# Scatter products of a mixture-of-experts tail on two PSUM banks, the output stored in quarters, the overflow flag read ahead of the loop

## The reference

```python
def moe_swiglu(h, w_router, w_gate, w_up, w_down):
    logits = (ht @ w_router).astype(jnp.float32)
    top_vals, top_idx = lax.top_k(logits, TOP_K)
    gates = jax.nn.softmax(top_vals, axis=-1)
    ...
    g = lax.ragged_dot(xs, w_gate, group_sizes)
    u = lax.ragged_dot(xs, w_up, group_sizes)
    y = lax.ragged_dot(jax.nn.silu(g) * u, w_down, group_sizes)
    y = y * gates.reshape(-1)[order][:, None].astype(y.dtype)
    out = jax.ops.segment_sum(y, tok, num_segments=t)
...
x = x + moe_swiglu(h, *p["ffn"])
```

## Time and profile before

| | |
|---|---|
| Median of 3 runs | 1593.89 us (1590.03, 1593.89, 1594.02) |
| Profiled execution, its own time | 1592.94 us |
| Profiled execution, span from first to last instruction | 1591.2 us |
| PE matmul busy | 1499.9 us (94%) |
| PE weight loads busy | 1205.7 us (76%) |
| DVE busy | 1151.8 us (72%) |
| ACT busy | 952.2 us (60%) |
| DMA, mean over the span | 268 GB/s |
| Largest share of the chain of waits | PE, line 646, 64% |

### The profile page before, as it was taken

How to read it: one execution, slowest core, us unless ns; L and a number is a source line. 1 busy time by engine, 2 the same in 40 slices (tenths; PEclk the granted TensorE clock), 3 DMA queues, 4 the chain that set the end, 5 groups by cost and what they waited for, 6 DMA issues and landing times.

```text
span 1591.2 us, 20133 instructions
## 1 busy us (share of the span) xinstructions
PE 1499.9 (94%) x7597; PEld 1205.7 (76%) x7597; DVE 1151.8 (72%) x1196; ACT 952.2 (60%) x922; POOL 68.3 (4%) x93
## 2 busy tenths in 40 slices
PE   6988979999887799999999999999999999999996
PEld 3677579999643578878878887887887887887884
DVE  6683225445254388888888888888888988888885
ACT  4323134444243377777777777776777767777773
POOL 2640000000010000000000000000000000000000
PEclk8998989999999799999999999999999999999997
DMA  7343924537430369989989999999999998998990
GB/s 235 113 42 97 350 106 162 183 109 262 159 106 1 106 237 368 375 307 364 372 326 345 372 339 336 368 337 337 369 337 336 369 371 304 367 375 308 363 367 28
DMA packets 197936, 425.92 MB, mean 268 GB/s; under 512 B 19331, under 2 KB 28385, under 8 KB 197857
## 3 DMA queue, kind: packets, MB, share of 16 engines
q1 hardware_dynamic: 197584, 425.23, 75.4%
q10 hardware_dynamic: 304, 0.06, 0.0%
HBM read 421.67 MB, written 1.05 MB: 266 GB/s over the span
## 4 chain that ended last, share of the span: by engine, by line
PE 82%; DVE 8%; ACT 6%; issue 3%; POOL 1%; ACTq 0%; DVEq 0%; POOLq 0%
PE bank L646 64%; PE bank L613 3%; PE bank L369 3%; PE bank L770 2%; PE bank L438 2%; PE bank L394 2%; ACT w_hi L1322 2%; PE bank L781 2%; DVE w_lo L1698 1%; PE bank L598 1%; PE bank L699 1%; PE bank L576 1%; ACT L1347 1%; DVE work L1535 1%; POOL work L1019 1%
## 5 line engine op out<-in xcount | busy, mean ns | idle before, releaser
L1698 DVE TENSOR_TENSOR w_lo<-ring,w_hi 128x2048 fp32r<-128x2048 f32 x342 | 780.5, 2291 | 124.6 <-ACT w_hi L1322 121.5
L1322 ACT ACTIVATE w_hi<-ring 128x2048 fp32r<-128x2048 f32 x342 | 652.4, 1917 | 143.8 <-PE bank L646 141.9
L646 PE MATMUL bank<-w_hi,xg_hl 128*128 128x512 f32 x1792 | 564.1, 396 | 2.7 <-DVE xg_hl L1752 2.7
L646 PEld LDWEIGHTS bank<-w_hi,xg_hl 128*128 128x128 f32 x1792 | 332.9, 188 | 77.5 <-issue 10.6
L646 PE MATMUL bank<-w_lo,xg_hl 128*128 128x512 f32 x896 | 350.0, 391 | 0.0
L646 PE MATMUL bank<-w_hi,at_hl 128*128 128x512 f32 x896 | 283.3, 397 | 0.0
L646 PEld LDWEIGHTS bank<-w_hi,at_hl 128*128 128x128 f32 x896 | 167.2, 188 | 39.2 <-issue 3.8
L646 PEld LDWEIGHTS bank<-w_lo,xg_hl 128*128 128x128 f32 x896 | 168.2, 188 | 36.1
L646 PE MATMUL bank<-w_lo,at_hl 128*128 128x512 f32 x448 | 175.7, 392 | 0.0
L1615 DVE TENSOR_TENSOR fpart_hl<-ring,fpart_hl 128x1024 fp32r<-128x1024 f32 x66 | 80.7, 1225 | 93.1 <-ACT fpart_hl L1253 92.6
L646 PE MATMUL bank<-ht_hl,fpart_hl 128*128 128x256 f32 x1056 | 129.3, 285 | 3.7 <-DVE ht_hl L1626 2.1
(11 more groups left out here) (215 smaller groups left out, 1044.0 us busy)
## 6 DMA issues: line engine op xcount, KB each, us to landing
ring<-in_l_moe_w_gate SPq DMA_DIRECT2D x58, 2048.0 KB, 7.9
ring<-in_l_moe_w_up SPq DMA_DIRECT2D x57, 2048.0 KB, 7.8
ring<-in_l_moe_w_down SPq DMA_DIRECT2D x56, 2048.0 KB, 8.0
ring<-in_l_ffn_w_gate SPq DMA_DIRECT2D x5, 2048.0 KB, 7.8
ring<-in_l_ffn_w_up SPq DMA_DIRECT2D x5, 2048.0 KB, 8.3
ring<-in_l_ffn_w_down SPq DMA_DIRECT2D x5, 2048.0 KB, 7.7
ring<-in_l_w_in SPq DMA_DIRECT2D x4, 2048.0 KB, 8.8
ring<-in_l_w_out SPq DMA_DIRECT2D x4, 2048.0 KB, 8.4
```

Of the source, the lines that this page charges most:

```text
L646: last = mm(p, lhsT=xs[a], rhs=ws[b], start=start and q == 0, stop=stop and q == 2, **kw)
L1322: ac(w_hi(n), at(e_slot(q) * SLOT + j * HALF, HALF), ACT.Copy).then_inc(S("hi"), 1)
L1698: tt(LO[e_slot(q)][:, j * HALF:(j + 1) * HALF], at(e_slot(q) * SLOT + j * HALF, HALF), w_hi(n).bitcast(fp), ALU.subtract).then_inc(S("lo"), 1)
```

## The change

Three things change. The scatter products behind the loop (where `bt` is None) use bank 6 for the first half of the tokens (m = 0) and bank 7 for the second; those inside the loop stay on bank 7. The flag is waited for and loaded into a register ahead of the main loop on PE, ACT, DVE and SP; the branch on it stays behind the loop. SP stores each quarter of x (128 tokens x 512 columns, 256 KB) when its addition is done, and waits for all four; the single store and the memset that releases it now belong to the second pass alone.

```diff
-                p = unit(pe, (key, "sc", n, m), 7, bt)
+                p = unit(pe, (key, "sc", n, m), 6 + m if bt is None else 7, bt)
...
-            passes("main", 0, NE)
             pe.wait_ge(S("flag"), 1)
             over = pe.value_load(flag[0:1, 0:1], min_val=0, max_val=1)
+            passes("main", 0, NE)
             with pe.If(over > 0):
...
-            passes("main", 0, NE)
             sp.wait_ge(S("flag"), 1)
             over = sp.value_load(flag[0:1, 0:1], min_val=0, max_val=1)
+            passes("main", 0, NE)
+            for n, m in SC_AT.values():
+                read_out(sp, (("main", "end"), "sc", n, m))
+                sp.dma_start(out[0, m * P:(m + 1) * P, n * 512:(n + 1) * 512],
+                             XS[:, m, n * 512:(n + 1) * 512]).then_inc(S("stored"), 16)
             with sp.If(over > 0):
                 first_items(Turn(NE - 1, 0), NE - 1, EARLY, NSLOT, "main")
                 passes("over", NE, PASSES * NE)
-            sp.wait_ge(S("x_final"), 1)
-            sp.dma_start(out[0].rearrange("(m p) n -> p m n", p=P), XS).then_inc(S("stored"), 16)
-            sp.wait_ge(S("stored"), 16)
+                sp.wait_ge(S("x_final"), 1)
+                sp.dma_start(out[0].rearrange("(m p) n -> p m n", p=P), XS).then_inc(S("stored_over"), 16)
+                sp.wait_ge(S("stored_over"), 16)
+            sp.wait_ge(S("stored"), 64)
...
-            passes("main", 0, NE)
             act.wait_ge(S("flag"), 1)
             over = act.value_load(flag[0:1, 0:1], min_val=0, max_val=1)
+            passes("main", 0, NE)
...
-            passes("main", 0, NE)
             dve.wait_ge(S("flag"), 1)
             over = dve.value_load(flag[0:1, 0:1], min_val=0, max_val=1)
+            passes("main", 0, NE)
             with dve.If(over > 0):
 
                 v.memset(GATE, 0.0).then_inc(S("gate_zero"), 1)
+                dve.wait_ge(S("stored"), 64)
                 passes("over", NE, PASSES * NE)
-            v.memset(vt[:, 8:9], 0.0).then_inc(S("x_final"), 1)
+                v.memset(vt[:, 8:9], 0.0).then_inc(S("x_final"), 1)
```

## The result

The changed kernel takes 1581.14 us in the median of six runs (1577.58 to 1582.49); the kernel before, run beside it, 1591.74 (1588.80 to 1594.02). The ratio is 0.9935, with a 95% interval of 0.9921 to 0.9948: faster by 8.3 to 12.6 us. In a later comparison of the same two programs it was 0.9947 (0.9929 to 0.9966), 5.4 to 11.3 us. The forecast was 1584.9 us with 1581.5 to 1589.2 as its range.

A forecast was written before the change was run, and what follows sets the result against it. PE was taken to bound the loop, and the sequence behind the last expert product to set the end. Savings of 4.65 + 0.9 + 2.5 = 8.05 us from 1592.94 gave 1584.9 us, range 1581.5 to 1589.2.

The forecast's parts named there:

- The bound and the place of the gain: Expert loop bound by PE and untouched by the change; all 8.05 us saved behind the last expert product.
- the last quarter lands sooner: Rival, at the final store: the last quarter lands no faster, or SP's branch takes its place; 1587.4 us, chance 0.16.
- the loop starts as far behind the flag as before: Rival, at the loop's start: flag read or moved code costs 0.9 to 3.1 us once; 1585.8 to 1588.0, chance 0.08.
- the banks overlap: Rival, at the scatter products behind the loop: banks don't overlap, 4.65 us lost; 1589.55 us, chance 0.08.
- no instruction packet moved in the loop: Rival, in the loop: shifted code brings instruction loading at each of eight jumps back, 19 us; 1604 us, chance 0.06.
- the reference of the forecast: Start of the sum: profiled execution of 1592.94 us, with the first scatter product behind the loop starting at 1572.58 as now.
- part of the way to the lowest run of before (-1.8 of 2.9): Term of the range's low end, 1581.5 us, beside an early clock (-0.5) and a landing in 2.4 us (-1.1).
- Part 1, 4.65 us: Scatter products behind the loop on banks 6 and 7 run without a gap in 5.9 us; 4.65 us saved (3.4 to 5.15).
- the early end that I had kept: In the scatter block: full clock back 3.6 us in, so the block ends 5.4 us after its start, at 1578.0.
- Part 2, 0.9 us: From product 4's end to the store's issue 0.78 us instead of 1.67; 0.9 saved, moved reads cost 0.
- Part 3, 2.5 us: Store in quarters: the last lands in 3.5 us (2.4 to 6.0) instead of 6.0; 2.5 us saved.
- What is late next: At the end: SP's branch over the second pass, between its last issue and last wait, costs 0.5 us at most.

The follow-up runs named there:

- after_again: The changed kernel once more, with no edit: ratio 0.9947 to the kernel before.
- after_no_second: The changed kernel with the second pass (the branch and the code under it) left out on PE, ACT, DVE and SP: ratio 0.9940 to the kernel before.
- flag_only: The kernel before with only the flag's wait and load moved ahead of the loop on PE, ACT, DVE and SP: ratio 0.9987 to the kernel before.
- banks_only: The kernel before with only the four scatter products behind the loop on banks 6 and 7 in turn: ratio 0.9972 to the kernel before.
- one_store: The changed kernel with one store of the whole behind the last addition in place of four quarters: ratio 0.9958 to the kernel before.
- before_again: The kernel before once more, with no edit: ratio 0.9995 to the kernel before.

## Why the prediction was wrong, point by point

**The bound and the place of the gain** were right: the loop is bound by PE and did not change, and the 8.9 us lie in the tail. The rivals fell: the last quarter lands sooner, the loop starts as far behind the flag as before but for 0.3 us, the banks overlap, and no instruction packet moved in the loop (every packet between 700 and 1540 us was again data, 121501 of them).

**The step that failed is the reference of the forecast**, "it starts at 1572.58 as now", with the range built on it ("part of the way to the lowest run of before (-1.8 of 2.9)"). The first scatter product's start lies behind a part of 560 us whose length scatters, and the loop. One profile stood at 1572.58; with nothing but the flag's reads changed ahead of the loop it lay at 1568.75 and 1575.55 too. The execution that I summed against (1592.94) looked 0.95 us low against three runs; against the median of the six (1591.74) it was 1.2 us high. Of the 3.8 us between forecast and measurement this is 1.2. Another 0.8 is the tail (8.87 for 8.05), which the sum had too small. For the remaining 1.7 no trace shows a cause, and they are within the scatter: the second comparison gave the changed kernel 8.4 us and the first 10.3, with intervals that hold the tail's 8.4 to 8.9 both times. The range took 1.8 us for a low run on top of the best values of two terms; the interval of the first comparison, 2.1 us to each side, shows what the scatter alone asks for, whatever the terms.

**Part 1, 4.65 us:** measured 5.17 (10.57 less 5.40), and 5.0 in after_again. The order was as foreseen: no gap, and the clock back inside the block. It came back 3.7 us after the start, near the early end that I had kept. In after_no_second it took until 6.1, and the block 6.73 us. Over all profiles the block took 5.32 to 6.73 us, for the 5.4 to 7.17 of the text.

**Part 2, 0.9 us:** measured 0.9 (0.76 us from product 4 to the issue of the last store, for 1.67). The cost of the moved reads was 0, as said; flag_only shows it on its own. That it also keeps DVE's branch off the end was not among its uses: the prediction had DVE's end below the landing, which held by only 0.4 us.

**Part 3, 2.5 us:** measured 2.8, right in size by a wrong composition. The 3.3 us beside the data were not all a fixed part of the store: without the second pass the whole lands in 4.0 us and a quarter in 2.0. Their difference is 2.0 us, just the three quarters of data (0.75 x 2.67), and the fixed part is 1.3. The other 2.0 of the 6.0 us went away with the second pass and its instruction packets, and 1.2 to 1.6 of it still sits in the changed kernel's 3.2 and 3.6. The Trainium skill (DMA: Bandwidth & Descriptors, Anatomy of one DMA) has about 2.0 us of fixed part, fitted for DMAs that GpSimd issues; the stores here are SP's. As an estimate by it a quarter takes 2.7 us. The undisturbed one took 2.0, and the measurement decides.

**What is late next:** SP's branch cost nothing that shows; it waited for the landing 2.3 us. I had looked for the branch as time of an engine. The branches also cost through the store, a term that the prediction didn't have. The Trainium skill (Runtime: NRT & Kernel Launch, Instruction fetch mechanics) says that a taken branch to code that isn't loaded has it fetched by DMA first. The trace of the kernel before agrees, with one 16 KB and two 8 KB instruction packets between the store's issue and the end.

## What to carry to other kernels

At the end of a program nothing hides anything: read the chain from the last busy engine to the end row by row, and ask of every branch, flag read and memset whether it can stand earlier. Issue the output piece by piece as it is made; pieces that all wait for the last value cost more than one store (12.7 us against 11.1 in the traces). And before a gain of half a per cent is forecast from one profile, find how far the same program's landmarks move between runs: here the parts ahead of the change moved by more than most of its terms.

## What the runs showed of the hardware that was not expected

**A branch over unused code made a store slower.** The megabyte landed in 6.0 and 5.8 us in the kernel before, where a 16 KB instruction packet of 1.0 us came before the store's data were through, in 4.5 to 4.7 us where it came behind them (banks_only, flag_only, one_store), and in 4.0 without the second pass and its packets. In the first group PE met the block's end 0.7 to 0.8 us behind the store's issue, in the second 1.0 to 2.0 us. No run moved this packet alone.

**PE's clock depends on the idle time ahead.** After 2.7 us of idle time it was half at the start of the block, or fell within 0.35 us of it, in every profile of the table; after 0.73 us (both kernels with Y on ACT) or with the gap filled it stayed full into the products. How long it stayed half, in a block without gaps, differed by run: it was full again 2.9 to 3.7 us after the block's start in five profiles and 6.1 us in a sixth (after_no_second).

**The part ahead of the loop scatters with the clock, in part.** Two stretches from the start to the loop, of banks_only and of the changed kernel (columns as in the earlier trace rows):

```profile
0.00:563.00 563.00, 494.99 (x2998) 389.27 (x2998) 267.72 (x605) 209.89 (x377) 68.45 (x93) 0.92 0.45 143
```
```profile
0.00:556.30 556.30, 485.84 (x2998) 381.56 (x2998) 267.68 (x605) 209.94 (x377) 68.00 (x93) 0.94 0.45 145
```

The instructions are the same in number; PE was busy 9 us longer at the lower mean clock, and the loop began 6.7 us later. Between other pairs the clock does not account for the difference (before_again, like the kernel before, had 0.93 and PE busy for 4 us more, and began 0.4 us earlier), so the cause of the scatter stays open in part.
